# Moving the spread of the solved blocks from the end of one recurrence turn into the next

## What is computed

```
def step(S, inp):
    r_t, w_t, k_t, v_t, kk_t, a_t = inp
    sa = jnp.einsum('bhvk,bhk->bhv', S, -kk_t)
    S = S * w_t[:, :, None, :] + sa[..., None] * (kk_t * a_t)[:, :, None, :] + v_t[..., None] * k_t[:, :, None, :]
    return S, jnp.einsum('bhvk,bhk->bhv', S, r_t)
```

## Time and profile before

| what | value |
|---|---|
| median of 3 runs | 1779.41 us (1778.49 to 1782.28) |
| profiled execution | 1781.47 us |
| its span in the profile | 1779.8 us |
| PE busy | 92% of the span |
| PE weight loads busy | 73% |
| DVE busy | 60% |
| ACT busy | 22% |
| POOL busy | 9% |
| mean granted PE clock | 0.97 of full speed |

### The profile page before, as it was taken

One profiled execution on the slowest core, in us unless ns is written; L12 is line 12 of the kernel. 1 busy time (PEld: TensorE's weight loads), 2 busy tenths in 40 slices (PEclk: granted clock), 3 DMA queues, 4 the chain that ended last, 5 costly groups with the idle time before them and its releaser, 6 DMA issues.

```text
span 1779.8 us, 27649 instructions
## 1 busy us (share of the span) xinstructions
PE 1643.5 (92%) x9506; PEld 1296.3 (73%) x9506; DVE 1063.7 (60%) x5004; ACT 386.9 (22%) x966; POOL 161.4 (9%) x295
## 2 busy tenths in 40 slices
PE   8999988998999999888989989999999999999996
PEld 6877766766766667646987867777777777778895
DVE  3467567555555555435773466777777777431755
ACT  2011012111111121211112323333333333221011
POOL 1001122221212121210000000000000000020000
PEclk9999998999999999998999999999999999999998
DMA  9449999999999999987234232232323223364341
GB/s 380 168 161 378 401 417 399 411 421 385 411 379 420 418 420 387 385 340 283 102 149 171 89 108 98 98 99 99 99 98 102 97 80 113 107 254 177 129 157 50
DMA packets 101724, 419.94 MB, mean 236 GB/s; under 512 B 41796, under 2 KB 46288, under 8 KB 91984
## 3 DMA queue, kind: packets, MB, share of 16 engines
q0 software_dynamic: 41680, 218.91, 30.7%
q1 hardware_dynamic: 53256, 187.54, 28.0%
q10 hardware_dynamic: 6648, 11.73, 1.7%
HBM read 405.28 MB, written 12.85 MB: 235 GB/s over the span
## 4 chain that ended last, share of the span: by engine, by line
PE 58%; DMA 16%; DVE 14%; issue 4%; ACT 4%; SPq 2%; POOLq 1%; POOL 0%; ACTq 0%; DVEq 0%
PE psum L688 16%; PE psum L756 10%; DMA kvr<-in_cv 9%; PE psum L738 6%; PE psum L677 6%; PE psum L950 4%; PE psum L1089 3%; DMA kvr<-in_ck 2%; SPq L566 2%; DVE kmT L2277 2%; DVE kmT L2275 2%; PE psum L726 2%; PE psum L1136 2%; DMA kmT<-solved_t 1%; DVE kvr L1834 1%
## 5 line engine op out<-in xcount | busy, mean ns | idle before, releaser
L1834 DVE CUSTOM_DVE_ANT_0 kvr<-kvr,arena 128x128 f32<-128x128 f32 x1440 | 313.9, 286 | 167.4 <-DMA kvr<-in_ck 167.2
L688 PE MATMUL psum<-hT,wring 128*128 128x264 f32 x1408 | 336.7, 396 | 0.0
L688 PEld LDWEIGHTS psum<-hT,wring 128*128 128x128 f32 x1408 | 268.5, 194 | 63.0 <-issue 18.7
L1089 PE MATMUL psum<-hT,kvr 128*128 128x264 f32 x1152 | 283.9, 391 | 1.8 <-DVE hT L2182 1.8
L1089 PEld LDWEIGHTS psum<-hT,kvr 128*128 128x128 f32 x1152 | 214.3, 192 | 42.7 <-issue 8.9
L950 PE MATMUL psum<-kvr,arena 128*32 128x384 f32 x1024 | 106.3, 524 | 23.9 <-DMA kvr<-in_cv 23.9
L738 PE MATMUL psum<-hT,kvr 128*128 128x264 f32 x512 | 118.9, 387 | 0.0
L1834 DVE DVE_READ_ACCUMULATOR2_ANT arena<- 128x1 f32 x1440 | 117.4, 82 | 0.0
L738 PEld LDWEIGHTS psum<-hT,kvr 128*128 128x128 f32 x512 | 95.5, 190 | 16.0 <-issue 0.4
L625 POOL DMA_DIRECT2D kvr<-in_cv x128 | 68.0, 531 | 342.2 <-PE psum L950 245.4
L625 POOL DMA_DIRECT2D kvr<-in_ck x128 | 67.9, 530 | 293.4 <-issue 180.5
(11 more groups left out here) (417 smaller groups left out, 2346.4 us busy)
## 6 DMA issues: line engine op xcount, KB each, us to landing
kvr<-in_ck POOLq DMA_DIRECT2D x128, 768.0 KB, 13.0
kvr<-in_cv POOLq DMA_DIRECT2D x128, 768.0 KB, 12.5
kvr<-in_wrkv SPq DMA_DIRECT2D x12, 3072.0 KB, 14.2
kvr<-in_wo SPq DMA_DIRECT2D x14, 2048.0 KB, 8.2
wring<-in_wkv SPq DMA_DIRECT2D x12, 2048.0 KB, 11.7
wring<-in_wm SPq DMA_DIRECT2D x8, 2048.0 KB, 11.6
wring<-in_wg SPq DMA_DIRECT2D x8, 2048.0 KB, 12.3
kvr<-in_wg SPq DMA_DIRECT2D x8, 2048.0 KB, 8.9
```

What stands on the lines that cost most here:

```text
L688: last = mm(psum[:, m % 2, 0:n], w[:, k, t * P:(t + 1) * P], rhs[:, k, 0:n], start=(k == 0), stop=(k == KT - 1))
L1089: last = mm(psum[:, m % 2, 0:T], w[:, k, t * P:(t + 1) * P], hT[:, k, :], start=(k == 0), stop=(k == KT - 1))
L1834: last = v_.tensor_tensor_reduce(page, page, qb[:, n % 2, h * P:(h + 1) * P], 1.0, 0.0, ALU.mult, ALU.add, S[:, n % 2, j * FH + h:j * FH + ...
```

## The change

The DVE spreads the solved blocks of pair o not at the end of turn o - 1 but in turn o, behind the mix and the keys and ahead of the centring. The number of `fs` that it waits for is that of the same transfers as before, since `o` is now one larger. The call depends on `solve` now, where it stood in the branch of `prepare`; both hold for 12 turns. The other engines' programs are the same. The short description of the change also names the joining with the output projections by seven half-width products; the diff has nothing of that, and both kernels have such products in their output projections.

```diff
@@ -2281,7 +2281,7 @@
 
                 def diagonals():
 
-                    dve.wait_ge(sem("fs"), FS * (o + 2))
+                    dve.wait_ge(sem("fs"), FS * (o + 1))
                     on = masks[:, K_BM:K_BM + P].rearrange("p (b t) -> p b t", b=8).unsqueeze(1).to_broadcast([P, 8, 8, BLK])
                     tt(TU16.rearrange("p q (u b t) -> p (q u) b t", u=2, b=8),
                        TUc.rearrange("p q u t -> p (q u) t").unsqueeze(2).to_broadcast([P, 8, 8, BLK]), on, ALU.mult)\
@@ -2309,6 +2309,8 @@
                 if prepare:
                     mix()
                     keys()
+                if solve:
+                    diagonals()
                 if late:
                     centred()
                 if prepare:
@@ -2345,7 +2347,6 @@
                     dve.wait_ge(sem("z_y"), 2 * (o + 1) + 2)
                     ch.do(tt(x3(Z[:, 1, :]), x3(B), i64, ALU.mult))
                     v_.tensor_reduce(ys[:, a, :], x3(Z[:, 1, :]), AX.X, ALU.add).then_inc(sem("prepared"), 1)
-                    diagonals()
                 else:
                     scaled_state()
                 if solve:
```

## The result

| | before | changed |
|---|---|---|
| median of 5 runs each | 1782.28 us | 1767.96 us |
| ratio | 1 | 0.9928, 95% interval 0.9906 to 0.9949 |
| span of the profiled execution | 1779.8 us | 1765.6 us |

The changed kernel was measured twice more beside the kernel before: 0.9938 (0.9916 to 0.9960) and 0.9954 (0.9938 to 0.9970). The three ratios stand for 8, 11 and 13 us, and their intervals reach from 5 to 17.

What follows compares the result with a forecast made beforehand. Bound: each turn's path of PE outputs, DVE chain L2353 to L2206, then PE, with fetch and spread pushed in between. 5.3 + 3.8 + 0.8 = 9.9 us off 1781.47, less 2.1 for the runs' median: 1769.5 us, range 1765 to 1776.

Steps and rivals of the forecast that it cites:

- Turns 1 to 10: Output copies start right after the PE's outputs, no longer behind fetch and spread: 5.3 us gained, turns 3 and 10 losing.
- The spread's own price: 1.14 us a turn on the DVE chain, claimed not saved but moved from before the copy to behind the keys.
- Turn 0: First turn, no outputs before it: the DVE starts the mix instead of idling for the fetch, 3.8 us gained.
- Its lower bound: Least gain of turn 0, from the DVE starting L2233 earlier: 2.5 us.
- The 1.23 us at L2253: DVE's wait for ACT in turn 0, claimed to go too if the PE is early by more than 3 us.
- The clock: PE clock falls in the turns: one of the two later falls gone at half its price, 0.8 us gained.
- the PE's wait in front of the second L1240: PE's wait for the DVE's centring in turn 8: 1.33 us of waits become one piece of 0.6 us.
- Turn 7, in which the two were to meet: Widest turn: the PE's arrival at the second L1240 and the DVE's delivery were to meet there.
- The gain given back by a transfer: Rival: a transfer or ACT comes last in turns 1 to 10, only turn 0's gain stays, 1776 to 1777 us; chance 0.10.
- ACT, which I had 0.17 us from the path: ACT's table load in turn 8: could start at 1403.16 after the DVE's state, ACT being free at 1402.99.
- The clock falling in every turn: Rival: one-piece wait before L1240 brings eight more falls, 6 to 13 us lost, 1776 to 1783 us; chance 0.05.
- Slower by the spread's price: Rival: spread free at its old place, not behind the keys; 1.14 us a turn, 12.5 us, 1792 us; chance 0.03.

Runs made afterwards that it cites:

- e2: Changed kernel, with the DVE also waiting for the fetch at the old place, ahead of the output copies: 1779.77 us, 0.9998 of the kernel before.
- e3: Changed kernel, with the spread done twice at its new place: 1786.74 us, 1.0048 of the kernel before.
- e4: Kernel before, with only pair 0's spread moved into turn 0, the other eleven left at their turns' ends: 1774.85 us, 0.9977 of the kernel before.
- e1: Changed kernel measured again without any edit: 1768.02 us, 0.9938 of the kernel before.
- e11: Changed kernel measured a third time without any edit: 1769.23 us, 0.9954 of the kernel before.
- e7: Changed kernel, with ACT's six copies (L1682) moved behind the next turn's two sigmoids: 1767.34 us, 0.9923 of the kernel before.
- e9: Changed kernel, with the spread moved inside the keys, between L2225 and L2227: 1768.06 us, 0.9946 of the kernel before.
- e10: Changed kernel, with ACT's issue of the state's store moved behind its two sigmoids: 1767.64 us, 0.9944 of the kernel before.
- e5: Changed kernel, with the spread on GpSimd as soon as the blocks are fetched, none on the DVE: 1780.87 us, 0.9994 of the kernel before.
- e6: Changed kernel, with the spread moved ahead of the mix, behind the state: 1772.98 us, 0.9944 of the kernel before.
- e8: Changed kernel, with the spread on GpSimd and ACT's copies behind the sigmoids: 1777.92 us, 0.9981 of the kernel before.

## Why the prediction was right

The forecast was 1769.5 us, 9.9 us taken off the time before; it came to 1767.96 us, the profiles' turns say 11.0 us won (9.2 and 12.3 with the repeats), the three ratios 8 to 13. That the time came within 1.6 us is in part luck: the kernel before itself came out at 1779.41 us in three runs and at 1782.28 us in five. Step by step:

**Turns 1 to 10**, forecast 5.3 us, signs included: turns 3 and 10 lost 0.17 and 0.19 (forecast −0.16 and −0.20), turn 7 won 1.21 (1.41), turn 8 0.70 (0.73). Together they won 6.8 us. The 1.5 more is in turns 2 and 5, 0.79 us over the forecast of each: the two turns in which the clock had fallen. Without them it is 5.2 us for 5.3. Shown by e2: give the wait back, and the whole gain goes.

**The spread's own price isn't saved.** Shown by e3 for each of the turns at 1.25 us, and by the 7.04 against 5.88 us of the chain.

**Turn 0**, forecast 3.8, measured 3.95 to its second L1157, and alone in e4. Its lower bound, the DVE's own 2.5 us to L2233, came to 2.58. The 1.23 us at L2253, which the prediction let go because the PE is early, were the clock's work: in the kernel before, the granted clock was 0.50 in 1060 to 1062, the PE ran L1113 and L1157 in it, ACT's L1594 stood behind that L1157 and its exponentials behind L1594, and the DVE waited for them.

```profile
1059.36 1.25 PE L1113 MATMUL psum<-arena,cst 128*128 128x264 f32 x2 [0.49 <-DVE arena L2229]
...
1060.40 1.91 PE L1157 MATMUL psum<-vmr,gT 128*128 128x128 f32 x8
...
1062.35 0.60 ACT L1594 ACTIVATE arena<-psum 128x512 f32<-128x512 f32 x1 [3.05 <-PE psum L1157]
```

In the changed kernel L1113 and L1157 take 0.66 and 1.16 us, 1.34 us less together. An estimate from these rows is that without the fall the wait of 1.23 us would not have been there; no run shows turn 0 of the kernel before without it.

**The clock**, forecast 0.8 us as one fall less. All three falls went, and it was worth 0.79 us each in turns 2 and 5, 1.6 together; the term was half its size. With the estimated 1.2 us of turn 0 the clock has 2.8 of the 11.0 us. This is the part that luck has a say in: falls come in some turns and not in others that look alike, and a profile of the kernel before with more or fewer of them would have given another sum. One fall cost half of the 1.6 us that I had as its upper price; a part of the lost work lies in waits that the PE has anyway (the 0.25 us in front of the second L1157 is gone in turns 2 and 5 of the kernel before).

**A figure that failed:** the PE's wait in front of the second L1240. I had it at 0.6 us, and that it meets the DVE in turn 7. It is 1.23 us in all ten turns. I had taken the PE's arrival from its bracketed waits (0.65 and 0.68), but the PE loses more than these around a wait. From L1108 to L1113 it took 1.38 us in turn 8 with 0.68 us of listed wait, and takes 0.45 us now without one, so 0.25 us was not listed; from L1113 to L1240 it took 0.81 us with no wait listed at all. Turn 7, in which the two were to meet, has 1.23 us as well. Since the DVE comes last there anyway, the sum didn't suffer.

**The rivals.** The gain given back by a transfer: no; the DVE's other wait for one, for `near` at L2275, came to 12.3 us between 1060 and 1500 us, 12.1 before. ACT, which I had 0.17 us from the path, was on it by 0.2 us, before and after alike. The clock falling in every turn: the opposite. Slower by the spread's price: the point at which it decides, outputs later than the fetch, was met in turns 3 and 10 and cost 0.17 and 0.19 us, no more, since only the overlap counts.

## What to carry to other kernels

An in-order engine's wait for a slow round trip belongs behind all work that doesn't need its result. What it is worth can be read in advance: the wait's release minus the moment at which the next item's data were ready, summed over the turns, with the negative ones. Here that gave 5.3 us for a measured 5.2 without the clock's part. It holds only while no other engine comes last at the new place, which has to be read from the rows too. The work that is moved with the wait keeps its price as long as it stays in the same chain; e3, one repeat of it, measures that price.

Before an idle engine is given the work, look which operations of the busy one will run beside it: one small operation a turn, held for the length of GpSimd's, was enough to lose the whole gain.

## What the runs showed that I had not expected

The clock. In the profiles of the changed kernel and of e1, e11, e7, e9 and e10 the granted clock did not fall once in the turns 0 to 10, 66 turns. In the kernel before and e2 it fell nine times in 22 turns, in e3 six times in 11. In e4 and e5 it fell twice, in e6 once, in e8 four times. One thin stretch doesn't always bring a fall: in the changed kernel the PE's busy time can be as low as 0.77 of 2 us with the clock at 1.00:

```profile
1094.00:1096.00 2.00, 1.02 (x5) 0.35 (x3) 1.97 (x4) 0.55 (x2) 0.00 (x0) 1.00 0.75 319
...
1096.00:1098.00 2.00, 1.75 (x12) 1.65 (x13) 1.90 (x8) 0.00 (x0) 0.00 (x0) 1.00 1.00 430
...
1137.00:1139.00 2.00, 0.77 (x4) 0.33 (x3) 1.97 (x4) 0.39 (x1) 0.00 (x0) 1.00 0.92 393
```

The PE's listed waits don't explain it: up to the centring's L1240 they come to 12.3 us between 1060 and 1500 us in both kernels (4.3 at L1108, 6.6 at L1113 and 1.4 at the first L1240 before, all of it at the second L1240 after). But the list leaves out what the PE loses around a wait, as above. The time from the end of the outputs to the start of the second L1240 has the same PE work in it in all kernels, turn for turn, so its differences between kernels are the PE's real waiting. Summed over turns 1 to 10, beside the falls in them:

| kernel | sum | shortest, longest | falls |
|---|---|---|---|
| before | 76.6 us | 6.93, 8.54 | 2 |
| changed | 71.3 | 7.13, 7.13 | 0 |
| e1, e11, e7 | 72.0, 71.3, 71.3 | 7.12, 7.86 | 0, 0, 0 |
| e6, e9, e10 | 70.0, 69.4, 69.9 | 6.92, 7.28 | 0, 0, 0 |
| e4 | 75.8 | 6.77, 8.13 | 2 |
| e2 | 76.5 | 7.20, 8.17 | 5 |
| e5 | 78.3 | 7.55, 8.12 | 2 |
| e8 | 79.3 | 7.49, 9.22 | 4 |
| e3 | 84.2 | 8.38, 8.71 | 6 |

The changed kernel has 5.3 us less of it than the kernel before, which is the forecast of turns 1 to 10 again. One of the 21 falls (e8, turn 10) came inside this time, behind an idle piece of 1.64 us, and made it the 9.22 of the table. The other 20 came near its end, all of them in the 40 turns in which it was over 7.8 us; the other 20 of these held the clock, and so did all 89 shorter ones. So the falls go with longer waiting of the PE there, but why one long turn falls and the next doesn't stays open, and no run varied this time alone.

The Trainium skill, "TensorE: Matmul & The Clock Gate", "A second HAM failure mode: psum-queue depth-cycling", has frequent short idles as a cause, in a bf16 kernel. The trace agrees for the kernel before and e2, which have several a turn and fell. It doesn't bear out that their number decides: e3 has one of 2.49 us and at most one of 0.25 us in most of its turns and fell six times in turns 0 to 10, as e2 did, and e6 has two or three short ones in each of its turns 1 to 9 (0.49 us, 0.25 us and up to 0.40 us) and didn't fall there.

The other surprise was that a DVE copy of 8 columns stood for 1.91 us behind GpSimd (e5).
